# Seven half-slots of background weight products moved inside RWKV

## What is computed

```python
h = x + 0.5 * SwiGLU_1(RMSNorm(x))
proj = RMSNorm(h) @ w_in            # RWKV-7 columns, gated-DeltaNet columns, two gates of 2048
y_rw, y_gdn = rwkv7(proj[...]), gated_deltanet(proj[...])
h = h + (sigmoid(G_A) * (y_rw @ L_A) + sigmoid(G_B) * (y_gdn @ L_B)) @ w_out
h = h + cross_attention(RMSNorm(h), RMSNorm(mem))
h = h + 0.5 * SwiGLU_2(RMSNorm(h)); y = RMSNorm(h)
```

## Time and profile before

| | |
|---|---|
| median of three runs | 2590.79 us |
| profiled execution, its own time | 2591.7 us |
| its span, first to last instruction | 2590.0 us |
| PE busy | 2554.0 us, 99% |
| weight loads of PE | 2096.9 us, 81% |
| DVE busy | 1955.3 us, 75% |
| ACT busy | 1339.4 us, 52% |
| POOL busy | 194.3 us, 8% |
| mean DMA rate | 212 GB/s |
| chain that ended last: PE, DVE, issue | 83%, 9%, 3% |

### The profile page before, as it was taken

One profiled execution on the slowest core, in us unless ns is written; L12 is line 12 of the kernel. 1 busy time (PEld: TensorE's weight loads), 2 busy tenths in 40 slices (PEclk: granted clock), 3 DMA queues, 4 the chain that ended last, 5 costly groups with the idle time before them and its releaser, 6 DMA issues.

```text
span 2590.0 us, 34012 instructions
## 1 busy us (share of the span) xinstructions
PE 2554.0 (99%) x13547; PEld 2096.9 (81%) x13547; DVE 1955.3 (75%) x2315; ACT 1339.4 (52%) x1568; POOL 194.3 (8%) x354
## 2 busy tenths in 40 slices
PE   8999999999999999999999999999999999999998
PEld 7888888888888777777788888888888888887887
DVE  6888888887767796958766766555668888888876
ACT  5555555555556366446445544433455454555554
POOL 2000000000000010011001112000100000000000
PEclk9999999999999999999999999999999999999999
DMA  6767676667676575656588879643867677766655
GB/s 213 236 210 243 209 239 214 217 206 228 216 210 195 180 230 161 180 158 178 156 288 255 254 244 281 201 154 130 239 189 232 219 227 222 229 216 223 209 202 175
DMA packets 278703, 548.21 MB, mean 212 GB/s; under 512 B 25148, under 2 KB 35552, under 8 KB 278160
## 3 DMA queue, kind: packets, MB, share of 16 engines
q1 hardware_dynamic: 253904, 478.60, 58.2%
q0 software_dynamic: 24320, 66.90, 8.8%
q10 hardware_dynamic: 320, 0.53, 0.1%
HBM read 508.15 MB, written 37.77 MB: 211 GB/s over the span
## 4 chain that ended last, share of the span: by engine, by line
PE 83%; DVE 9%; issue 3%; ACT 2%; DMA 2%; POOL 0%; SPq 0%; DVEq 0%; ACTq 0%; POOLq 0%
PE pp L794 14%; PE pp L795 14%; PE pp L796 14%; PE pp L415 10%; PE pp L416 10%; PE pp L417 10%; DVE wlo L376 2%; PE pb L795 1%; PE pb L796 1%; PE pb L794 1%; PE pa L794 1%; PE pa L795 1%; PE pa L796 1%; ACT whi L371 1%; DMA raw<-in_ffn_w_up 1%
## 5 line engine op out<-in xcount | busy, mean ns | idle before, releaser
L376 DVE TENSOR_TENSOR wlo<-raw,whi 128x1024 fp32r<-128x1024 f32 (+1 forms) x764 | 919.9, 1216 | 347.9 <-ACT whi L371 328.9
L371 ACT ACTIVATE whi<-raw 128x1024 fp32r<-128x1024 f32 (+1 forms) x764 | 798.0, 1053 | 623.4 <-PE pp L417 440.1
L794 PE MATMUL pp<-whi,xhi 128*128 128x512 f32 x1040 | 404.7, 389 | 0.0
L796 PE MATMUL pp<-wlo,xhi 128*128 128x512 f32 x1040 | 404.7, 389 | 0.0
L795 PE MATMUL pp<-whi,xlo 128*128 128x512 f32 x1040 | 404.7, 389 | 0.0
L415 PE MATMUL pp<-whi,xhi 128*128 128x512 f32 (+1 forms) x928 | 370.4, 399 | 0.7 <-DVE xlo L533 0.7
L416 PE MATMUL pp<-whi,xlo 128*128 128x512 f32 (+1 forms) x928 | 359.4, 387 | 0.0
L417 PE MATMUL pp<-wlo,xhi 128*128 128x512 f32 (+1 forms) x928 | 359.3, 387 | 0.0
L847 ACT ACTIVATE whi<-tw 128x1024 fp32r<-128x1024 f32 x124 | 131.6, 1062 | 280.5 <-PE pp L796 119.3
L794 PEld LDWEIGHTS pp<-whi,xhi 128*128 128x128 f32 x1040 | 195.3, 188 | 40.6
L795 PEld LDWEIGHTS pp<-whi,xlo 128*128 128x128 f32 x1040 | 195.3, 188 | 40.6
(11 more groups left out here) (528 smaller groups left out, 3671.2 us busy)
## 6 DMA issues: line engine op xcount, KB each, us to landing
raw<-in_ffn_w_gate SPq DMA_DIRECT2D x176, 512.0 KB, 4.5
raw<-in_ffn_w_up SPq DMA_DIRECT2D x176, 512.0 KB, 4.7
raw<-in_ffn_w_down SPq DMA_DIRECT2D x176, 512.0 KB, 4.5
raw<-in_w_in SPq DMA_DIRECT2D x144, 512.0 KB, 4.4
hid_dram<-hid_t POOLq DMA_DIRECT2D x43, 512.0 KB, 5.2
xq<-hid_dram POOLq DMA_DIRECT2D x156, 128.0 KB, 3.5
raw<-in_w_lift SPq DMA_DIRECT2D x32, 512.0 KB, 5.7
raw<-in_w_out SPq DMA_DIRECT2D x32, 512.0 KB, 4.9
```

What stands on the lines that cost most here:

```text
L371: nc.scalar.activation(whi[:, s, :, 0:width], raw[:, r % RING, :, 0:width], ACT.Copy).then_inc(whi_ready, 1)
L376: nc.vector.tensor_tensor(wlo[:, s, :, 0:width], raw[:, r % RING, :, 0:width], whi[:, s, :, 0:width].bitcast(F32), ALU.subtract).then_inc( ...
L794: nc.tensor.matmul(out, a_hi, whi[:, s, block, :], start=start, stop=False)
L796: return nc.tensor.matmul(out, a_hi, wlo[:, s, block, :], start=False, stop=stop)
```

## The change

Only the three tables change. For PE, `STEPS` gets one half-slot at `bonus_out` and one more at `nat` in both RWKV halves, and three more at `rw0.y`. These seven half-slots are no longer done in "rest". ACT and DVE get one more slot each at `rw0.y`.

```diff
-    "rw0.lora": 4, "rw0.g": 10, "rw0.kk": 7, "rw0.tilde": 10, "rw0.nat": 1, "rw0.mats0": 4, "rw0.mats1": 4,
+    "rw0.lora": 4, "rw0.g": 10, "rw0.kk": 7, "rw0.tilde": 10, "rw0.bonus_out": 1, "rw0.nat": 2, "rw0.mats0": 4, "rw0.mats1": 4,
...
-    "rw0.y3": 8, "rw0.y": 3,
+    "rw0.y3": 8, "rw0.y": 6,
...
-    "rw1.lora": 4, "rw1.g": 11, "rw1.kk": 5, "rw1.tilde": 10, "rw1.nat": 1, "rw1.mats0": 4, "rw1.mats1": 4,
+    "rw1.lora": 4, "rw1.g": 11, "rw1.kk": 5, "rw1.tilde": 10, "rw1.bonus_out": 1, "rw1.nat": 2, "rw1.mats0": 4, "rw1.mats1": 4,
...
-    "rw0.y3": 1, "rw0.out": 1, "rw0.y": 3,
+    "rw0.y3": 1, "rw0.out": 1, "rw0.y": 4,
...
-    "rw0.y1": 1, "rw0.y2": 1, "rw0.out": 2, "rw0.std": 1, "rw0.y": 2,
+    "rw0.y1": 1, "rw0.y2": 1, "rw0.out": 2, "rw0.std": 1, "rw0.y": 3,
```

## The result

The changed kernel takes 2611.83 us (2607.91 to 2613.21, five runs) against 2590.79 before (2588.73 to 2592.89, by now over five runs too). The ratio over the runs is 1.0071, with a 95% interval of 1.0058 to 1.0083: **slower by 0.7%**. (The medians alone lie 21.0 us apart, a quotient of 1.0081.) The forecast was slower, 2609, with a range of 2600 to 2617.

A forecast was written before the change was run, and what follows sets the result against it. PE was taken to set the time, changed only by its idle time and clock. Delays less 9.5 gave +16.7, the clock +1.9: 18.6 on 2591.7 is 2610.3, or 2609 against the median; range 2600 to 2617.

The forecast's parts named there:

- "rest": Slot 127 is written 6.7 us behind L2002 and wanted at 2.2: 4.6 idle, delay +26.2; then 9.5 comes off.
- the clock: Idle stretches of 4.9, 3.9 and 4.6 us may lower PE's clock: 3.8 us in all or 0; half taken, 1.9.
- y3: Half 1: slot 126 is written behind r_out, so the stage takes 12.6 us instead of 9.9; delay +21.6.
- Half 0: Five half-slots, 6.8 us, are done for nothing; delay 0.0 when PE starts the gate stage of half 1.
- The early waits: Half 1, g and kk: PE waits for slots 97 and 102, L1910 starts at 28.1 instead of 24.1; delay +4.0.
- mats0, mats1, inverse: Half 1: PE waits for slots 111, 113, 115 and 117, which DVE writes late; delays +7.8, +12.3 and +18.9.
- slot 117: Inverse of half 1: written behind the spreading at 16.2 us, three half-slots before L1341; stage 20.6 instead of 14.0.
- ACT's copies of finished blocks: Two come one place earlier in ACT's order: 0, or 1 us if one lands badly.
- The first rival: Subtractions are in time everywhere, so only gains are left, 8.5 us: 2582; chance 0.08.
- The rival with late weights: Low-rank weights land 2 or 3 us later, wait and low clock stay; up to 4 us more, 2613; chance 0.12.

The follow-up runs named there:

- e8: Changed kernel without the two half-slots at bonus_out and nat of half 1, with one slot more of ACT and DVE at rw1.lora; 2588.64 us, ratio 0.9983.
- e1: Changed kernel, PE's table untouched, ACT and DVE slots brought forward at rw1.lora, inv3.row14 (DVE only) and rw1.y; 2585.72 us, ratio 0.9972 to the kernel before.
- e10: The kernel of e1 run once more beside a new set of runs of the kernel before; 2586.84 us, ratio 0.9972.
- e3: Changed kernel without the two half-slots at bonus_out and nat of half 1, supply as changed; 2599.88 us, ratio 1.0025 to the kernel before.
- e4: Kernel before with only the two half-slots at bonus_out and nat of half 1, supply untouched; 2594.92 us, ratio 1.0007.
- e5: e2 with one of DVE's two slots at inv3.blocks done at inv3.row14 instead; 2590.80 us, ratio 0.9993 to the kernel before.
- e7: Changed kernel with one slot more of ACT and DVE at rw1.lora and nothing else; 2591.93 us, ratio 1.0002 to the kernel before.
- e9: e2 with both DVE slots of inv3.blocks done at inv3.row14 and that of inv3.20 at rw1.r0; 2590.10 us, ratio 0.9989 to the kernel before.
- e2: Kernel before with only the three half-slots at rw0.y and one slot more of ACT and DVE there; 2592.40 us, ratio 0.9996.

## Why the prediction was right

The mechanism held by its own steps: the gain up to the gate products of half 1, and then one wait after another for slots that DVE writes later in its chain. That the total came as close as it did is in part luck, since the clock took more than was counted and `y3` less. Below, the delay of PE at a place, start after less start before:

| place | predicted | measured |
|---|---|---|
| L1887, half 1 | +1.7 | +1.3 |
| first background matmul behind the gate products | 0.0 | -0.2 |
| L1910 | +4.0 | +3.8 |
| L1922 | +4.7 | +4.2 |
| L1935, first | +5.0 | +4.6 |
| L1935, second | +7.8 | +8.3 |
| L1304 | +12.3 | +13.5 |
| L1341 | +18.9 | +21.0 |
| L2002 | +21.6 | +22.4 |
| end of "rest" | +16.7, with the clock +18.6 | +18.9 |

- **Half 0** gains as said: five half-slots for a delay of -0.2 us, the load wait and the low clock at the low-rank products gone. e8 has these moves alone, fed, and gains too.
- **The early waits** are 1.07 and 2.22 us plus two that hold a start up by under 0.2, against 1.3 and some 2.4. They were sized from rows of before whose anchor is the gate product, and the anchor held.
- **mats0, mats1, inverse**: 2.49, 4.44 and 3.76 idle, against 2.8, 4.9 and 3.9. At slot 117 a wait of 2.8 was part of my sum and none is there. PE came to it late, since the clock was low over slot 115 and 116, but only 0.3 us behind DVE's subtraction, so DVE's time would have set the stage without that. The sum has a slip here: 20.6 is counted from DVE's first row of substitution (1230.67) and the 14.0 of before from PE's first background matmul (1230.18). From the same row before has 13.5, so the step is +7.1 and not +6.6, and the forecast should have been 0.5 higher. Measured from DVE's row the stage is 20.65. At `mats0` the stage took 11.4 us for 10.4; 0.6 of it is a stall of "issue" inside L1935.
- **y3** was sized too high: the stage grew by 1.5 us, not 2.7. Its wait is that for slot 124, 1.46 us; slot 126 was written 9.6 behind the stage's start instead of 11.0, before PE asked for it. I had called the earlier place of ACT's copies of finished blocks worthless. One of them left the path to `r_out` and shortened it.
- **"rest"**: 4.28 idle for 4.6. In all L415 waits 19.7 us for wlo in half 1, where the prediction had some 23; the 2.8 of slot 117 is most of the difference.
- **The clock** was the loosest term. In the profiled execution it fell after all three long waits, and stood low for 3.4, 6.8 and 3.4 us. (The rule weighed in the prediction, from the Trainium skill's page TensorE: Matmul & The Clock Gate, Part 1, had all three fall; the trace agrees with it there.) From the distances at half clock the first cost 1.6 us, half of it ahead of L1304. The second cost 0.3, as PE would otherwise have waited for slot 117 instead, and the third 1.6. That is 3.5 us where the sum has 1.9, and it makes most of the delays at L1304 and L1341 beyond the sum. The median run may have lost more: this execution has a mean clock of 0.997 and 2607.91 us, the lowest of the five; the other four have 0.995 and 2609.3 to 2613.2. That the spread between them is the clock is argued from these numbers, not shown in a trace.
- Behind "rest" the profiled execution won back 2.6 us (1324 to 2590 before, 1343 to 2606 after). The profile of before has waits of 1.0, 0.6 and 1.3 us far behind RWKV that this one lacks. Other profiles have them or not, also of the same kernel (e1 and e10), and no edit reaches that far.

The first rival asked for a supply that keeps up. It was wrong about this kernel, and e1 shows that it names the cure: with DVE's order brought forward as in its diff the time comes to 0.9972, where that rival had 2582 of 2590.8, 0.9966. The rival with late weights is out too: L1887 of half 1 has no wait.

## What to carry to other kernels

Where two engines walk the same numbered work by separate tables, a step added in one table shifts every number behind it. Before filling a wait, list for each slot the place that makes it and the place that uses it, and look for makers that stand behind something the user's engine has yet to release: those waits no spare time covers. Move the maker with the user. Here one slot of DVE and ACT at the right place was worth 19 us in the profiled stretch, and the moves themselves, well fed, some 6 to 8.

## What the runs showed that was not expected

- The low clock does not need an idle stretch as long as the 3.51 us of the earlier trace rows. It fell behind stalls of 1.14 (e3), 1.6 (e4 and e5) and 2.03 us (e8), behind waits of 2.38 (e7 and e9), and behind 2.22 in e3 but not behind the same 2.22 in the changed kernel, nor behind 2.49 there. So the length of one idle stretch does not tell whether the clock falls. The falls lasted 3.4 or 6.8 us, and one of 3.4 cost up to 1.7. A short stall in a dense stretch can cost twice its length or more (1.14 and 1.7 in e3).
- PE can run out of instructions. Inside L1341, whose 256 small matmuls take 6.35 us, it stood still for 1.1 to 3.0 us in five of the ten profiles of experiments, with no semaphore to wait for, until 1.2 to 1.5 us behind the end of a 16 KB instruction fetch. In e2 that took back nearly all that the change had gained. PE's order sets where it stops; that the weight loads beside it set how long is argued.
